# Latent attention: normalising a head's sums instead of its exponents, with four buffers of turned rows and values loaded by pair of heads

## What is computed

```python
def chunk_causal_attention(q, k, v):
    ...
    def block(args):
        qi, i = args
        s = jnp.einsum('bqhd,bkhd->bhqk', qi, k, preferred_element_type=jnp.float32) * scale
        q_chunk = (i * Q_BLOCK + jnp.arange(Q_BLOCK)) // CHUNK
        mask = key_chunk[None, :] <= q_chunk[:, None]
        pr = jax.nn.softmax(jnp.where(mask, s, -jnp.inf), axis=-1).astype(v.dtype)
        return jnp.einsum('bhqk,bkhd->bqhd', pr, v)
```

## Time and profile before

| | us |
|---|---|
| median of 3 runs (3256.7 to 4896.74) | 3258.41 |
| the profiled execution | 3251.87 |
| its span, first to last instruction | 3250.2 |
| latent attention within it, 370.6 to 551.8 | 181.2 |

### The profile page before, as it was taken

One profiled execution on the slowest core, in us unless ns is written; L12 is line 12 of the kernel. 1 busy time (PEld: TensorE's weight loads), 2 busy tenths in 40 slices (PEclk: granted clock), 3 DMA queues, 4 the chain that ended last, 5 costly groups with the idle time before them and its releaser, 6 DMA issues. The chain is left out here.

```text
span 3250.2 us, 37250 instructions
## 1 busy us (share of the span) xinstructions
PE 2927.2 (90%) x13724; PEld 2253.5 (69%) x13724; DVE 2068.6 (64%) x1970; ACT 1465.4 (45%) x1563; POOL 486.0 (15%) x495
## 2 busy tenths in 40 slices
PE   4998898999998779999997979998998659999993
PEld 3884355666666558888885757886776548888883
DVE  4888565121117768898984644235775578888984
ACT  3112454111112158787774431114663247777773
POOL 0004400000000011111111201007633100000002
PEclk8999899999999889999998989998999869999996
DMA  6112321010207456995215311110004559999995
GB/s 253 45 39 71 129 60 40 36 71 36 90 26 260 150 212 247 404 409 220 82 57 187 120 65 39 46 33 1 27 1 164 211 190 391 398 390 400 399 384 198
DMA packets 113974, 534.65 MB, mean 164 GB/s; under 512 B 15728, under 2 KB 27760, under 8 KB 74048
## 3 DMA queue, kind: packets, MB, share of 16 engines
q1 hardware_dynamic: 93904, 462.53, 37.2%
q0 software_dynamic: 15840, 57.68, 5.5%
q10 hardware_dynamic: 4112, 12.85, 1.0%
HBM read 561.47 MB, written 65.91 MB: 193 GB/s over the span
## 5 line engine op out<-in xcount | busy, mean ns | idle before, releaser
L1777 DVE TENSOR_TENSOR upper_split<-arena,upper_split 128x2048 fp32r<-128x2048 f32 x186 | 415.3, 2286 | 63.3 <-ACT upper_split L1723 63.2
L3136 DVE TENSOR_TENSOR upper_split_experts<-arena,upper_split_experts 128x2048 fp32r<-128x2048 f32 x144 | 328.8, 2292 | 45.8 <-ACT upper_split_experts L3090 44.5
L1723 ACT ACTIVATE upper_split<-arena 128x2048 fp32r<-128x2048 f32 x186 | 342.8, 1914 | 5.2 <-PE banks L177 5.2
L3090 ACT ACTIVATE upper_split_experts<-arena 128x2048 fp32r<-128x2048 f32 x144 | 275.4, 1917 | 95.3 <-PE banks L177 95.3
L175 PE MATMUL banks<-upper_split_experts 128*128 128x512 f32 x768 | 305.4, 398 | 13.2 <-DVE upper_split_experts L3136 13.2
L175 PE MATMUL banks<-upper_split 128*128 128x512 f32 x744 | 297.7, 400 | 11.7 <-DVE upper_split L1777 11.1
L177 PE MATMUL banks<-upper_split_experts 128*128 128x512 f32 x768 | 302.2, 393 | 0.0
L176 PE MATMUL banks<-upper_split_experts 128*128 128x512 f32 x768 | 302.0, 393 | 0.0
L177 PE MATMUL banks<-upper_split 128*128 128x512 f32 x744 | 292.3, 393 | 0.0
L176 PE MATMUL banks<-upper_split 128*128 128x512 f32 x744 | 292.2, 393 | 0.0
L1140 DVE TENSOR_TENSOR upper_latent<-arena,banks 128x512 f32<-128x512 f32 x48 | 33.0, 687 | 339.1 <-PE banks L1085 338.1
(11 more groups left out here) (449 smaller groups left out, 6255.7 us busy)
## 6 DMA issues: line engine op xcount, KB each, us to landing
arena<-in_exp_up_k SPq DMA_DIRECT2D x124, 1024.0 KB
arena<-in_gate_up SPq DMA_DIRECT2D x96, 1024.0 KB, 8.3
arena<-in_exp_down_k SPq DMA_DIRECT2D x62, 1024.0 KB
arena<-in_down SPq DMA_DIRECT2D x48, 1024.0 KB, 7.3
upper_middle<-in_gate_up SPq DMA_DIRECT2D x32, 1024.0 KB, 8.3
upper_middle<-in_down SPq DMA_DIRECT2D x16, 1024.0 KB, 6.7
y<-arena POOLq DMA_DIRECT2D x31, 512.0 KB, 2.9
arena<-in_merge_w SPq DMA_DIRECT2D x8, 1536.0 KB, 7.6
```

Source lines behind the costliest of these rows:

```text
L1723: a.activation(rounded(high[s]), raw[s], ACT.Copy).then_inc(high_made[up], 1)
L1777: v.tensor_tensor(rounded(low[s]), raw[s], plain(high[s]), ALU.subtract).then_inc(low_made[up], 1)
L3090: a.activation(rounded(high[n % RING]), raw[n % RAW], ACT.Copy).then_inc(high_made, 1)
L3136: v.tensor_tensor(rounded(low[n % RING]), raw[n % RAW], plain(high[n % RING]), ALU.subtract).then_inc(low_made, 1)
```

## The change

The exponents are turned and summed as they are, and each head's result is multiplied by the reciprocal of its exponents' sums. After the turn the queries lie along the columns, so the reciprocals have to be laid along them too: VectorE copies each reciprocal over 64 columns for each head (`widen`), TensorE multiplies by the identity to turn them (`flip`, bank 7), ScalarE copies the result to SBUF (`lay`, `rows`), and `keep` becomes a product. The sums use bank 6 alone. There are four buffers `pt`, and the values are loaded for one pair of heads at a time, two buffers of 128x8x128, in pieces of 512 B.

```diff
-    pt = [core.place(m["free"] + i * S, NT, P) for i in range(2)]
+    wide, rows = core.place(at + 2 * S + 16, P), m["root_rows"]
+    pt = [core.place(m["free"] + i * S, NT, P) for i in range(4)]
+    vt = [core.place(m["free"] + (4 + i) * S, NT, P) for i in range(2)]
...
         @block.sync
-            for t in range(NT):
-                sp.dma_start(vt[:, t, :], m["v1"][t]).then_inc(v_loaded[t], 16)
+            def load_values(it):
+                if it >= 2:
+                    sp.wait_ge(summed, NT * (it - 1))
+                sp.dma_start(vt[it % 2], m["v1"][:, :, it * P:(it + 1) * P].rearrange("t p d -> p t d"))\
+                  .then_inc(v_loaded[it % 2], 16)
+
+            load_values(0)
+            load_values(1)
             sp.wait_ge(h_low, ND)
             for it in range(1, NH1 // 2):
                 if it >= 2:
                     sp.wait_ge(scored, N * (it - 1))
                 for j in range(2):
                     load_heads(sp, m, 2 * it + j, it % 2, j)
+                if it >= 2:
+                    load_values(it)
...
             def turn(g):
-                pe.wait_ge(normed, g + 1)
+                pe.wait_ge(exped, g + 1)
...
+            def flip(x):
+                pe.wait_ge(spread, x + 1)
+                if x:
+                    pe.wait_ge(flat, x)
+                pe.matmul(ps[:, 7, 0:P], wide, core.col("ident"), start=True, stop=True).then_inc(flipped, 1)
+
             def sums(x):
                 pe.wait_ge(moved, 2 * x + 2)
-                if x >= 2:
-                    pe.wait_ge(kept, x - 1)
+                if x:
+                    pe.wait_ge(kept, x)
...
                 turn(g)
                 if g % 2 == 0 and g:
+                    flip(g // 2 - 1)
                     sums(g // 2 - 1)
+            flip(G // 2 - 1)
             sums(G // 2 - 1)
...
         @block.vector
-            def normalise(g):
-                _, i, j = where(g)
-                v.wait_ge(exped, g + 1)
-                c.step(v.reciprocal(rec[:, j:j + 1], den[:, j:j + 1]))
-                row = e[j][:, 0:(i + 1) * P]
-                v.tensor_scalar(row, row, rec[:, j:j + 1], None, ALU.mult).then_inc(normed, 1)
+            def widen(x):
+                here = rec[:, 2 * (x % 2):2 * (x % 2) + 2]
+                v.wait_ge(exped, 2 * x + 2)
+                if x:
+                    v.wait_ge(flipped, x)
+                c.step(v.reciprocal(here, den[:, 2 * (x % 2):2 * (x % 2) + 2]))
+                v.tensor_copy(wide.rearrange("p (j d) -> p j d", j=2),
+                              here.unsqueeze(2).to_broadcast([P, 2, 64])).then_inc(spread, 1)
...
-                v.tensor_copy(oT[:, it, i * P:(i + 1) * P], ps[:, 6 + x % 2, 0:P]).then_inc(kept, 1)
+                v.wait_ge(flat, x + 1)
+                v.tensor_tensor(oT[:, it, i * P:(i + 1) * P], ps[:, 6, 0:P], rows, ALU.mult).then_inc(kept, 1)
...
             for g in range(G):
                 if g + 2 < G:
                     bias(g + 2)
-                if g + 1 < G:
-                    normalise(g + 1)
-                if g % 2 == 0 and g >= 4:
-                    keep(g // 2 - 2)
-            keep(G // 2 - 2)
+                if g % 2:
+                    widen(g // 2)
+                    if g >= 3:
+                        keep(g // 2 - 1)
             keep(G // 2 - 1)
...
         @block.scalar
             def exp(g):
+                if g >= 4:
+                    a.wait_ge(spread, g // 2 - 1)
...
             def move(g):
                 a.wait_ge(turned, g + 1)
-                if g >= 2:
-                    a.wait_ge(summed, g // 2)
+                if g >= 4:
+                    a.wait_ge(summed, g // 2 - 1)
...
+            def lay(x):
+                a.wait_ge(flipped, x + 1)
+                if x:
+                    a.wait_ge(kept, x)
+                a.activation(rows, ps[:, 7, 0:P], ACT.Copy).then_inc(flat, 1)
...
                 move(g)
+                if g % 2 == 0 and g:
+                    lay(g // 2 - 1)
+            lay(G // 2 - 1)
```

More of the change, by code:

```diff
@@ L846, in latent_attention @@
 def latent_attention(core, m):
-    nc, ps, vt, oT = core.nc, core.ps, m["vt"], m["oT"]
+    nc, ps, oT = core.nc, core.ps, m["oT"]
     sem = lambda n: core.semaphore("at_" + n)
     q_loaded = m["q_loaded"]
-    v_loaded = [sem(f"v{t}") for t in range(NT)]
-    scored, biased, exped, normed, turned, moved, summed, kept, steps, h_high, h_low = map(sem, (
-        "scored", "biased", "exped", "normed", "turned", "moved", "summed", "kept", "steps", "h_high", "h_low"))
+    v_loaded = [sem(f"v{x}") for x in range(2)]
+    scored, biased, exped, spread, flipped, flat, turned, moved, summed, kept, steps, h_high, h_low = map(sem, (
+        "scored", "biased", "exped", "spread", "flipped", "flat", "turned", "moved", "summed", "kept", "steps",
+        "h_high", "h_low"))
     at = UPPER + 4 * S
@@ L920, in sums @@
                 pe.wait_ge(moved, 2 * x + 2)
-                if x >= 2:
-                    pe.wait_ge(kept, x - 1)
-                if it == 0:
-                    pe.wait_ge(v_loaded[i], 16)
+                if x:
+                    pe.wait_ge(kept, x)
+                if i == 0:
+                    pe.wait_ge(v_loaded[it % 2], 16 * (it // 2 + 1))
                 for t in range(i + 1):
                     for j in range(2):
-                        h = 2 * it + j
-                        ins = pe.matmul(ps[64 * j:64 * j + 64, 6 + x % 2, 0:P], vt[:, t, h * VH:(h + 1) * VH],
-                                        pt[j][:, t, :], start=(t == 0), stop=(t == i), skip_group_check=True)
+                        ins = pe.matmul(ps[64 * j:64 * j + 64, 6, 0:P], vt[it % 2][:, t, j * VH:(j + 1) * VH],
+                                        pt[2 * (x % 2) + j][:, t, :], start=(t == 0), stop=(t == i),
+                                        skip_group_check=True)
                 ins.then_inc(summed, 1)
@@ L963, in keep @@
                 v.wait_ge(summed, x + 1)
-                v.tensor_copy(oT[:, it, i * P:(i + 1) * P], ps[:, 6 + x % 2, 0:P]).then_inc(kept, 1)
+                v.wait_ge(flat, x + 1)
+                v.tensor_tensor(oT[:, it, i * P:(i + 1) * P], ps[:, 6, 0:P], rows, ALU.mult).then_inc(kept, 1)
             bias(0)
             bias(1)
-            normalise(0)
             for g in range(G):
@@ L982, in exp @@
                 _, i, j = where(g)
+                x = 2 * (g // 2 % 2) + j
                 a.wait_ge(biased, g + 1)
@@ L985, in exp @@
                     a.wait_ge(turned, g - 1)
+                if g >= 4:
+                    a.wait_ge(spread, g // 2 - 1)
                 a.activation(e[j][:, 0:(i + 1) * P], flat2(ps, 2 * j)[:, 0:(i + 1) * P], ACT.Exp,
-                             bias=nb[:, j:j + 1], scale=scale, accum_out=den[:, j:j + 1]).then_inc(exped, 1)
+                             bias=nb[:, j:j + 1], scale=scale, accum_out=den[:, x:x + 1]).then_inc(exped, 1)
             def move(g):
@@ L991, in move @@
                 a.wait_ge(turned, g + 1)
-                if g >= 2:
-                    a.wait_ge(summed, g // 2)
-                a.activation(pt[j].rearrange("p a b -> p (a b)")[:, 0:(i + 1) * P], flat2(ps, 4)[:, 0:(i + 1) * P],
-                             ACT.Copy).then_inc(moved, 1)
+                if g >= 4:
+                    a.wait_ge(summed, g // 2 - 1)
+                a.activation(pt[g % 4].rearrange("p a b -> p (a b)")[:, 0:(i + 1) * P],
+                             flat2(ps, 4)[:, 0:(i + 1) * P], ACT.Copy).then_inc(moved, 1)
+            def lay(x):
[3 more added lines that the diff above has]
+                a.activation(rows, ps[:, 7, 0:P], ACT.Copy).then_inc(flat, 1)
             exp(0)
@@ L3295, in build @@
             core.open_upper(own, "upper_attention", F32, m["free"])
-            m["vt"] = core.place(at(45440), NT, HALF)
+            m["root_rows"] = core.place(at(16448), P)
             run(latent_attention, m)
```

## The result

| | before | after |
|---|---|---|
| median of the runs, us | 3257.62 (5 runs) | 3237.45 (5 runs, 3236.09 to 3239.89) |
| ratio, 95% interval | | 0.9949 (0.9939 to 0.996) |
| span of the profiled execution | 3250.2 | 3235.8 |
| latent attention in it | 181.2 | 163.0 |
| first scores to first sums / to sums n = 5 | 7.7 / 36.3 | 7.7 / 27.9 |

The time fell by 0.5%, 17 us by the ratio; the two medians stand 20.2 apart. One of the five runs before took 4896.74 us, and the ratio leaves it out. 14.1 us and 3244 us were forecast, in a range of 3232 to 3259; the cases had 0.96 on a change within 2%.

The account below looks back on a forecast made before the run. TensorE was taken to bound the stage, with 5.3 us of waits per steady quarter. Quarter gains 6 + 1.5 + 1.5 + 3.6, plus 1.5 for the first quarter's n = 6 to 8, gave 14.1 us: 3244 us, range 3232 to 3259.

Parts of the forecast that it names:

- n = 7: Interval between starts of sums ending at seven key blocks, steady quarter: 7.03 us to fall near 6.0, gain 1.0.
- Steady quarters: Second and third quarters of latent attention: 40.9 us to fall to 39.4, gain 1.5 us each.
- n = 2 to 6: Among the six intervals besides n = 7 and 8: flips cost 1.5 us, 0.6 of 1.9 waits remain, net -0.2.
- 1.71+0.12+0.75+0.02+0.21+0.12+0.86+0.02 = s+3.8: At n = 7, TensorE reaches the flip 3.8 us after s, the start of the second head's scores for n = 8.
- n = 8: Interval between starts of sums ending at eight key blocks: 5.52 us to 4.8, gain 0.7, the turn's copy wait staying.
- First quarter: Latent attention's first quarter, up to sums n = 5: gain 4.8 to 7.5 us by when the clock rises, 6 taken.
- Rival 3: First quarter: widen's copy waits beside POOL as L959 did, 4 us less gain, 3248 us; chance 0.12.
- The end: Last sums n = 7 to the stage's end: gain 3.8 us; n = 1 to 6 -0.2, so quarter 4 gains 3.6.
- a difference outside the stage: Any difference outside latent attention, listed among the signs that the prediction was wrong.
- Rival 1: Slower: flips at 0.55 us on TensorE and late widen and keep turn the gain to -2 us, 3260; chance 0.12.
- rival 2: First quarter gives nothing up to n = 5 because the clock rises later: 8 us gain, 3250; chance 0.13.
- Rival 4: More: clock rises already at n = 2, small n lose their waits: 22 us gain, 3236; chance 0.13.

Follow-up runs that it names:

- The double flip: Changed kernel with every flip made twice into the same bank: steady quarter 40.5 us against 38.7, 169.0 us to the last sums against 160.7.
- the transpose: Changed kernel with the flip as a transpose instead of a product: steady quarter 37.8 us against 38.7, runs' ratio to the kernel before 0.9936.
- the copies by bank: Changed kernel with ScalarE's copy of a turned row made and released bank by bank for n of 5 to 8: steady quarter 37.2 us against 38.7.
- the run without GpSimd: Changed kernel with TensorE waiting for GpSimd's whole split before its first scores: first quarter 43.9 us against 45.5.

## Why the prediction was right, and where it was off

*What bounds.* Right. The count of TensorE's work gave n = 6 of before within 0.02 us and left the waits at n = 7 and 8 to be named; the 1.9 us in the other six intervals it left unnamed. The double flip and the transpose moved the quarter by TensorE's price of a product.

*Steady quarters.* Forecast 39.4 us, measured 38.7, by two errors of opposite sign. For n = 2 to 6 I was 0.2 to 0.3 us too long each, 1.2 in all: I had charged 0.12 us from scores to turn for both heads as a change-over. The rows after show 0.12 for the second head (479.34 to 480.95 for 7 blocks) and 0.01 for the first (481.61 to 483.33 for 8): for the first it had been a short wait for the normalisation. The trace before has TensorE's weight load of this turn waiting for it:

```profile
494.12 0.74 PEld L914 LDWEIGHTS banks<-arena,upper_latent 128*128 128x128 f32 x7 [0.81 <-DVE upper_latent L959]
```

And the flip takes the place of a change-over of 0.16 between turn and sums with one of 0.01 before it and 0.11 behind it, so it costs 0.17, not 0.25. For n = 7 I was 0.5 too short (6.0, measured 6.53). The step that failed is the count "1.71+0.12+0.75+0.02+0.21+0.12+0.86+0.02 = s+3.8": it let the turn of n = 8 follow the scores of n = 1 at once, though the wait for the copy of the turn before (0.75 + 0.22 + 0.92) was due there as it was at n = 8, where I did count it. With the copies by bank, where that wait is gone, n = 7 took 5.91. n = 8 (4.8, measured 4.76) and n = 1 (4.25, measured 4.26) came out as worked.

*First quarter.* Forecast 6 us up to n = 5, with 4.8 to 7.5 between its two readings; measured 8.4. The low end, 4.8, and the high one, 7.5, both let the first sums come 0.4 us earlier than before, without a reason; they came as late (7.7). The clock rose 12 us into the stage, some 0.5 us before sums n = 2, where I had it in n = 3. But n = 2 took 4.97 us where I counted 6.0, and most of that ran at half rate: of the difference the clock explains some 0.4, and the rest is a term that I had too large, the change-overs, 1.07 in the 6.0. The rows show 0.19 from sums to scores, 0.17 from scores to turn for the second head, nothing measurable for the first, and 0.11 from flip to sums. Rival 3's mechanism was there: two copies stood behind GpSimd for 1.67 and 1.53 us, and the flip waited 0.97 for the second (390.02). The Trainium skill (SBUF — State Buffer, "Who interferes with whom") has the rule of the port pair shared with GpSimd, under which, of two instructions that need it, the later waits for the whole of the other; the trace agrees, also for a source that repeats (1.67 us, ended 0.08 after GpSimd's). But its price was 1.6 us, by the run without GpSimd, not 4. I had called the clock and the lock two causes; the experiment says that the lock came first, 9.7 us with the later clock in them.

*The end.* Forecast 3.8 us from the last n = 7 on. From sums n = 6 to the end of the stage it was 15.85 before (535.90 to 551.75) and 12.7 after: 3.2. It is short by the same missed wait, 1.10 us there. And 1.3 of the gain, forecast and measured, is the half clock in the sums of the earlier trace rows: I took the end of before with it and my own without, and gave no reason why it should not come again. It did, behind the stage.

*Sum.* Forecast to the profile's measure: 6, 1.5, 1.5, 1.5, 3.6; measured 8.4, 1.2, 2.2, 2.2, 4.1. The sum was 4 us low, half of it in the first quarter (2.1), and outside the stage the profile gave 3.8 back, which I had put at nothing. The prediction names a difference outside the stage as a sign of being wrong; the rows show 2.1 of it as a later start behind the same code, and 1.6 as the half clock. That the forecast for the profiled execution, 3237.8, was met by 3237.45 is luck: two errors of 4 us that cancel. By the ratio of the runs the change is worth 17 us, 14.1 forecast.

Rival 1 is out by the price of a flip, rival 2 by the clock at 385. Rival 4 was nearer than I had allowed: the clock was up before n = 2 had ended, and n = 1 to 6 gave 0.9 us a steady quarter, where I forecast -0.2 and it had 1.1. The 3244 for the runs also carried 6.5 us by which the median of before stood above its profile; the profiled execution after is itself the median, so that 3237 lies near rival 4's 3236 says little by itself.

*What was not foreseen* is how the parts divide. I had credited n = 7 to the moved normalisation and n = 8 to the buffers. n = 8 does come with the buffers alone. And n = 7 does come with the moved normalisation alone. But for n = 1 to 6 neither part gives anything alone. At n = 4 the rows show why, the other's link then holds the same work; for the other n it is taken from their intervals, not read one by one.

## What to carry to other kernels

Where two links end nearly together at one instruction, taking either away can move nothing while taking both away moves the time; test them singly and together before dropping one. When one wait is worked out of a recurrence, put every other semaphore of the same instruction through the same sum at every step, not only where the trace shows it waiting. And a short SBUF-to-SBUF copy on VectorE beside a stream of long GpSimd instructions can cost what is left of theirs (1.67 us here), not its own 0.23: keep it off the path or ahead of what waits.

## What the runs showed of the hardware

A copy whose source repeats each of two elements 64 times is held behind GpSimd's instruction (1.67 and 1.53 us for 0.23), as the normalisation of a plain row was (2.46 us for 0.35). The clock, kept up to the start of the stage by unused products, fell again within 4 us, TensorE having been busy 0.69 of the first 2, and the filling bought nothing in the changed kernel (27.9 us to n = 5 with and without). On TensorE a float32 transpose of 128 columns takes half of the product that moves the same data, 0.107 us for 0.213, and lowered the quarter by that difference eight times.
